# An interleaved second projection, per-token scales held in the constants' tile, and a head norm spread over the recurrence's tiles

## The reference, cut to what matters

```
h_lat = layernorm(x) * (1 + scale) + shift        # 512 tokens, x is the first block's RMS-normed output
h_ctx = the same for 256 context tokens           # computed earlier, loaded from memory
p = h @ w_in                                      # 5*512 columns get a 3x3 (or 3-tap) convolution,
                                                  # the rest: values mv, output gate mo, gates, low-rank lw, la, lg
out_m = sigmoid(mo) * headnorm(mLSTM(...))        # one mixer: chunkwise recurrence, both directions merged
out_r = (headnorm(rwkv7_scan(...)) + bonus) * g   # the other mixer: a second recurrence
x = layernorm(alpha * x + gate * ([out_m, out_r] @ w_out)) ...   # alpha = 2 ** 0.25
```

## Time and profile before

| | us |
|---|---|
| three runs, median (lowest to highest) | 3100.05 (3097.63 to 3113.56) |
| the profiled execution, its own time | 3105.09 |
| its span (first to last instruction) | 3102.8 |
| busy: PE / DVE / ACT / POOL | 2879.1 / 1863.6 / 1257.7 / 793.4 |
| second projection, first latent matmul to last copy's start | 1597.99 to 1850.70 |
| recurrence, first matmul to last sum | 2023.54 to 2369.89 |

### The profile page before, as it was taken

One profiled execution on the slowest core, in us unless ns is written; L12 is line 12 of the kernel. 1 busy time (PEld: TensorE's weight loads), 2 busy tenths in 40 slices (PEclk: granted clock), 3 DMA queues, 4 the chain that ended last, 5 costly groups with the idle time before them and its releaser, 6 DMA issues. The chain is left out here.

```text
span 3102.8 us, 55532 instructions
## 1 busy us (share of the span) xinstructions
PE 2879.1 (93%) x22953; PEld 2326.6 (75%) x22953; DVE 1863.6 (60%) x2647; ACT 1257.7 (41%) x1624; POOL 793.4 (26%) x461
## 2 busy tenths in 40 slices
PE   9889999999999989999989899768999799999994
PEld 7467888799777767888858677567886478888883
DVE  3766663210344445565257957785654789998997
ACT  3544322221333343332244312512222277777775
POOL 2013444344222203444400000010100125354431
PEclk9999999999999999999989899889999799999997
DMA  4633422332211112222222100321003379999996
GB/s 169 233 134 121 96 95 95 111 111 94 82 55 69 69 42 109 95 95 98 99 103 82 55 33 2 140 84 44 31 31 121 130 292 365 364 377 364 360 372 266
DMA packets 83397, 440.96 MB, mean 142 GB/s; under 512 B 19712, under 2 KB 22784, under 8 KB 34816
## 3 DMA queue, kind: packets, MB, share of 16 engines
q1 hardware_dynamic: 73920, 429.63, 38.2%
q0 software_dynamic: 9280, 8.43, 0.8%
HBM read 423.30 MB, written 37.77 MB: 149 GB/s over the span
## 5 line engine op out<-in xcount | busy, mean ns | idle before, releaser
L85 POOL TENSOR_TENSOR ring_lo<-ring,unit_hi 128x2048 fp32r<-128x2048 f32 x110 | 507.2, 4611 | 1047.5 <-ACT unit_hi L74 1047.5
L146 PE MATMUL wide<-h_hi,unit_hi 128*128 128x512 f32 x1296 | 516.7, 399 | 13.4 <-DVE h_lo L566 5.0
L148 PE MATMUL wide<-h_hi,ring_lo 128*128 128x512 f32 x1296 | 507.7, 392 | 0.0
L147 PE MATMUL wide<-h_lo,unit_hi 128*128 128x512 f32 x1296 | 507.0, 391 | 0.0
L3317 DVE TENSOR_TENSOR ex_w_lo<-ring,ex_w_hi 128x2048 fp32r<-128x2048 f32 x194 | 442.1, 2288 | 48.4 <-ACT ex_w_hi L3312 47.3
L3312 ACT CAST ex_w_hi<-ring 128x2048 fp32r<-128x2048 f32 x194 | 369.5, 1908 | 120.0 <-DMA ring<-in_weights 106.3
L74 ACT CAST unit_hi<-ring 128x2048 fp32r<-128x2048 f32 x114 | 217.6, 1909 | 389.6 <-PE wide L148 384.4
L146 PEld LDWEIGHTS wide<-h_hi,unit_hi 128*128 128x128 f32 x1296 | 245.0, 189 | 73.8 <-issue 15.2
L148 PEld LDWEIGHTS wide<-h_hi,ring_lo 128*128 128x128 f32 x1296 | 244.8, 189 | 52.5
L147 PEld LDWEIGHTS wide<-h_lo,unit_hi 128*128 128x128 f32 x1296 | 245.4, 189 | 49.1 <-issue 0.2
L391 DVE TENSOR_TENSOR ffn_hidden_lo<-ffn_whole,ffn_hidden_hi 128x512 f32 (+1 forms) x44 | 201.3, 4575 | 51.0 <-ACT ffn_hidden_hi L366 51.0
(11 more groups left out here) (560 smaller groups left out, 5770.5 us busy)
## 6 DMA issues: line engine op xcount, KB each, us to landing
ring<-in_weights SPq DMA_DIRECT2D x356, 1024.0 KB, 6.1
rw_F<-factors SPq DMA_DIRECT2D x8, 1024.0 KB, 6.0
factors<-rp_out SPq DMA_DIRECT2D x4, 1280.0 KB, 5.3
factors<-rp_out SPq DMA_DIRECT2D x4, 1024.0 KB, 5.1
ex_both<-pair_rows_out SPq DMA_DIRECT2D x4, 1024.0 KB, 7.8
x<-in_x SPq DMA_DIRECT2D x8, 256.0 KB, 7.0
x_kept<-x SPq DMA_DIRECT2D x1, 2048.0 KB, 12.2
x<-x_kept SPq DMA_DIRECT2D x1, 2048.0 KB
```

What stands on the lines that cost most here:

```text
L85: pool.tensor_tensor(self.lo[n % RING][:, :], self.ring[n % RING][:, :], self.hi[n % 2][:, :].bitcast(F32), ALU.subtract).then_inc(self.lo ...
L146: pe.matmul(dst, a[0], b[0], start=start, stop=False)
L147: pe.matmul(dst, a[0], b[1], start=False, stop=False)
L148: return pe.matmul(dst, a[1], b[0], start=False, stop=stop)
```

## The change

1. *Entry.* The four clearings go to POOL. The first low half of the weights is written before the variance. The variance's root comes first. The power of x is not inverted as a 128x512 tile: TensorE transposes it (four transposes in bank 7), ScalarE takes the root of four columns, one for each token tile, into `c.x_cols`, which lies in columns of the constants' tile that are not used any more, and VectorE inverts them and multiplies by alpha. x is scaled by the gain alone, by ScalarE, behind chunk `lw` (`gains`), and by the column much later in place of L3126's alpha.
2. *Projection.* The order of the chunks is `mixed`, `lw`, `conv` 0 and 1, then `mo` or `lg` and `conv` by turns, then `conv` 7 to 19 (`PROJECTED`); the weights are packed in that order. The context matmuls of chunks 0 and 1 come before the latent ones, and those are interleaved over k with h's low halves. Units are cast and their low halves written one item earlier. The gates' arithmetic starts at chunk 6. The values no longer wait for the copy of the last chunk and use banks 6, 7, 0 to 3; the gates' transposes use banks 4 and 5.
3. *Recurrence.* The head norm of the other mixer moves to tiles 1 to 4, one token tile in each: four parts behind slots 1 to 4, the root in slot 10, the scaling behind slot 11. The 16 transposes are in slot 14 and the mixes in slots 16 and 17 of tile 5. `starts` of tile 1 waits for masked pairs of tile 0 in place of the mixes; the last chain waits for the mixes. The squares use U[0] in place of base[0].

```diff
     def tensor(self, pe):          # Entry
+        pe.wait_ge(self.power_ready, 1)
+        for t in range(TT):
+            mm = pe.transpose(self.c.bank[7][:, t * P:(t + 1) * P], self.x_scale[:, t * P:(t + 1) * P], self.c.ident[:, :])
+        mm.then_inc(self.power_turned, 1)
     def scalar(self, act, between):
         between()
-        act.wait_ge(self.power_ready, 1)
-        act.activation(self.x_scale, self.x_scale, ACT.Sqrt).then_inc(self.power_root_ready, 1)
         act.wait_ge(self.var_ready, 1)
         act.activation(self.z_scale, self.z_scale, ACT.Sqrt).then_inc(self.var_root_ready, 1)
+        act.wait_ge(self.power_turned, 1)
+        act.activation(self.c.x_cols, self.c.bank[7][:, 0:T:P], ACT.Sqrt).then_inc(self.power_root_ready, 1)
+    def gains(self, act):
+        for k in range(DC):
+            act.activation(self.x[:, k, :], self.x[:, k, :], ACT.Copy, scale=self.gain(k)).then_inc(self.x_ready, 1)
...
-GATES_AT = 1
+GATES_AT = 6
+PROJECTED = [("mixed", 0), ("lw", 0), ("conv", 0), ("conv", 1)]
+for m, kind in enumerate(("mo", "mo", "mo", "mo", "lg")):
+    PROJECTED += [(kind, m % MC), ("conv", m + 2)]
+PROJECTED += [("conv", m) for m in range(7, CONV_CHUNKS)]
...
+            for n in range(2):                         # tensor: context first, then latent by k
+                for k in range(DC):
+                    block(n, unit, k, con(n), context)
+            for k in range(DC):
+                pe.wait_ge(entry.h_lo_ready, k + 1)
+                for n in range(2):
+                    mm = block(n, unit, k, lat(n), latent)
...
-                if n >= 2 and n % 2 == 0:              # scalar
-                    w.write_hi(act, 0, n // 2 + 1)
+                if n % 2 == 1:
+                    w.write_hi(act, 0, n // 2 + 2)
...
+                while following <= min((n + 1) // 2 + 1, U_IN_COLUMNS):      # vector
+                    w.write_lo(dve, 0, following)
+                    following += 1
...
-                        pe.wait_ge(mixed_ready, MC)    # rwkv, starts of tile 1
+                        pe.wait_ge(pair_masked[d], NH)
...
-                            elif at == 12:
+                            if p == TAT - 1 and at == 14:
                                 turn_hidden()
...
-                            if p == 0:
-                                if at in (2, 4, 6, 8):
-                                    center_hidden(at // 2 - 1)
...
+                            if 1 <= p <= TT:
+                                if 1 <= at <= 4:
+                                    center_hidden(p - 1, at - 1)
+                                elif at == 11:
+                                    scale_hidden(p - 1)
+                            if p == TAT - 1 and at in (16, 17):
+                                for m in range(2 * (at - 16), 2 * (at - 16) + 2):
+                                    mix_hidden(m)
...
-                    act.mul(normed[:, n // 2, n % 2 * T:(n % 2 + 1) * T], c.bank[5][:, :], ALPHA)
+                    act.activation(normed[:, n // 2, n % 2 * T:(n % 2 + 1) * T], c.bank[5][:, :], ACT.Copy, scale=c.x_cols[:, n // 2:n // 2 + 1])
```

More of the change, by code:

```diff
@@ L1313, in vector @@
         dve.wait_ge(self.power_root_ready, 1)
-        dve.reciprocal(self.x_scale, self.x_scale).then_inc(self.x_scale_ready, 1)
+        dve.reciprocal(self.c.x_cols, self.c.x_cols).then_inc(self.x_scale_ready, 1)
         dve.wait_ge(self.x_scale_ready, 1)
[L1316 to L1319, removed]
+        dve.tensor_scalar(self.c.x_cols, self.c.x_cols, ALPHA, None, ALU.mult).then_inc(self.x_scale_ready, 1)
 ORDER = ([0, 1, 2, 3, 4, 5], [1, 0, 5, 4, 3, 2])
@@ L1437, in tensor @@
             a, t = n // TAT, n % TAT
-            pe.matmul(c.bank[6 + n // 9][:, n % 9 * GR:(n % 9 + 1) * GR], self.g.rows[a][0:GR, t * P:(t + 1) * P],
+            pe.matmul(c.bank[4 + n // 9][:, n % 9 * GR:(n % 9 + 1) * GR], self.g.rows[a][0:GR, t * P:(t + 1) * P],
                       c.ident[0:GR, 0:GR], start=True, stop=True).then_inc(self.turned, 1)
 def project_in_stage(nc, c, w, h, u, pads, entry, gates, constants):
-    items = [("mixed", 0), ("lw", 0), ("lg", 0)] + [("mo", m) for m in range(MC)] + [("conv", m) for m in range(CONV_CHUNKS)]
-    CONV_FIRST = len(items) - CONV_CHUNKS
+    items = PROJECTED
+    VALUE_BANKS = [c.bank[n] for n in (6, 7, 0, 1, 2, 3)]
     chunk_done, copied, convolved, v_copied_act, v_copied_dve, silu_done, ones_written, constants_loaded, blank, *rest = c.semaphores(
@@ L1499, in _, with block @@
             entry.tensor(pe)
+            def block(n, unit, k, dst, toks):
+                b = (n % 2 * DC + k) * P
+                return product(pe, dst, [part[:, b:b + P] for part in unit], [part[k][:, toks] for part in h], k == 0, k == DC - 1)
+            latent, context = slice(CTX, TA), slice(0, CTX)
+            unit = w.parts(pe, 0, 0)
+            pe.wait_ge(entry.loaded, 16 * len(entry.loads))
+            for n in range(2):
[5 more added lines that the diff above has]
+                    mm = block(n, unit, k, lat(n), latent)
+                    if k == DC - 1:
+                        mm.then_inc(w.used if ends[n] else chunk_done, 1)
             for n, (kind, m) in enumerate(items):
+                if n < 2:
+                    continue
                 if n % 2 == 0:
                     unit = w.parts(pe, 0, n // 2)
+                if n == 3:
+                    pe.wait_ge(entry.power_root_ready, 1)
                 if n >= 4:
                     pe.wait_ge(copied, n - 3)
-                parts = [(lat(n), slice(CTX, TA))]
-                if kind in ("mixed", "lw") or kind == "conv" and not latent_only(m):
-                    parts.append((con(n), slice(0, CTX)))
+                parts = [(lat(n), latent)] + ([(con(n), context)] if kind == "conv" and not latent_only(m) else [])
                 for dst, toks in parts:
-                    if n == 0 and toks.start == 0:
-                        pe.wait_ge(entry.loaded, 16 * len(entry.loads))
                     for k in range(DC):
[L1513 to L1516, removed]
+                        mm = block(n, unit, k, dst, toks)
                 mm.then_inc(w.used if ends[n] else chunk_done, 1)
-            pe.wait_ge(copied, len(items))
+            pe.wait_ge(copied, len(items) - 1)
             for k in range(DC):
@@ L2505, in turn_hidden @@
                     pe.wait_ge(normed, TT)
+                    for d in both:
+                        pe.wait_ge(s_ready[d], TAT)
                     for m in range(MC):
@@ L3860, in second_block_units @@
         mixed[:, 32 * q:32 * q + NH] = gates[:, group * NH:(group + 1) * NH]
-    yield by_column_chunk(np.concatenate([mixed, lw_f, lw_b, lg, mo, w_in[:, :5 * DM], np.zeros((D, P), w_in.dtype)], 1))
+    chunks = {"mixed": mixed, "lw": np.concatenate([lw_f, lw_b], 1), "lg": lg, "mo": mo, "conv": w_in[:, :5 * DM]}
+    projected = [chunks[kind][:, m * P:(m + 1) * P] for kind, m in PROJECTED]
+    yield by_column_chunk(np.concatenate(projected + [np.zeros((D, P), w_in.dtype)], 1))
     yield by_row_chunk(mv)
```

122 lines of the change are left out of this document (62 added, 60 removed).

## The result

The changed kernel took 3078.1 us (median of 4 runs, 3075.4 to 3081.9) beside 3101.6 us for the kernel before on the same chip: a ratio of 0.9922 (95% interval 0.9896 to 0.9949), 23.5 us faster. A second set on another occasion gave 3073.2 us (6 runs) against 3103.6, ratio 0.9901 (0.9877 to 0.9924), 30.4 us faster. The forecast was 3068 with a range of 3057 to 3084.

What follows compares the result with a forecast made beforehand. TensorE, busy 93% of the span, was taken as the bound, so gains come from its waits and slow stretches. Projection 20.7 plus net recurrence 12.2 is 32.9 us off 3100.05: forecast 3068, range 3057 to 3084 for 8 in 10.

Steps and rivals of the forecast that it cites:

- Entry: Before the projection: weight half 0 and memsets leave the variance's way, and its root goes first; gain 0.5 us.
- rival C: Projection: the context part doesn't run early, held by transposes or loads, costing 5.7 us; 3074 us in all; chance 0.05.
- The queue walk: Projection, engine queues followed in program order: TensorE idles 15.3 us, the stage ends at 1830 against 1850.7, gain 20.7 us.
- the low clock after the 4.8 wait is eaten by the next one: Projection, behind unit 12's wait: slow matmuls there cost nothing extra; only 2.6 us charged behind the later 7.4 us wait.
- A delay at the gains passes 1:1 to the end: Projection: any delay at ScalarE's eight gains on x (4.8 us in all) lengthens the stage by as much.
- rival A: VectorE's queue eats more of the projection: walk off by 8 us, first pair 4 later; 3080 us; chance 0.18.
- Tile 0: Recurrence: 14 slots fall from 37.9 to 22.2 us without the norm, 2.5 of it allowed for low clock; gain 15.7.
- Tiles 1 to 4: Recurrence: the norm's parts fit VectorE's idle times and cost nothing; 16 us if all were exposed.
- rival B: The norm parts are exposed in the recurrence's tiles 1 to 4: 16 us dearer, 3084 us; chance 0.06.
- Tile 5: Recurrence: sixteen transposes take 2.0 us and the mixes lengthen their slots by 0.65 each; cost 3.5 us.
- rival D: Projection: TensorE's clock stays low, 0.20 us more per 512-column matmul; 3107 us with fifteen chunks; chance 0.04.
- faster by more: Whole kernel under 3084.5 us, beyond 0.5%: forecast, a larger-gain rival, nearly all of rival A, half of rival B; 0.89.

Runs made afterwards that it cites:

- the mean of six: Six profiles of kernels holding the changed recurrence: it takes 323.0 to 329.0 us, mean 325.6, against 335.3 and 335.4 with the old recurrence.
- the fill: Chunk 0's context part computed twice and tile 5's mixes one per step, against the kernel with norm centring also in tile 0: 3059.1 us, ratio 0.9856.
- the gates early: Changed kernel with the gates' VectorE arithmetic moved from behind conv 10 to 14 to behind conv 1 to 5: 3057.7 us, ratio 0.9862.
- The three small edits: Added in turn to the gates early: gains behind conv 0's copies (3059.9 us); norm centring in tile 0 (3057.4); repeated context matmuls with mixes spread out (3059.1).
- the burst: 1512 independent matmuls (64, 8, 256 columns) before the recurrence, added to the gates early with gains behind conv 0's copies; 8 and 64 columns: 29 ns per recorded matmul.
- steps of 1.60 us: Two useless VectorE products in each of tile 0's steps 1 to 12, added to the gates early with gains behind conv 0's copies: thirteen steps 21.9 us against 20.6.

## Why the prediction was right, point by point

It had the direction, the main mechanisms and the range right; the gain was put at 32.9 us and is 23.5 and 30.4 in two sets. Summed from stretches it is 0.4 + 17.7 - 0.7 (the same in both profiles of the changed kernel) + 9.8 (the mean of six) = 27.2. The 5.7 us that are missing from 32.9 are 2.5 in the projection, 2.4 in the recurrence, 0.7 between the two and 0.1 in the entry.

- **Entry**: 0.5 said, 0.4 measured. The context part ran in the wait for the low half, so rival C is out. The first pair of chunks was put at 1608.3, or 1605.7 with this execution's head start of 2.6 us, and ended at 1607.8 (its last matmul starts at 1607.37): the prediction named the low clock as the risk, at 3 to 4 us; it was 1.6, shown by the fill that removed it.
- **The queue walk**: every late unit was named in its place. Idle 15.3 said, 11.5 measured (unit 13 did not wait). The failed step is "the low clock after the 4.8 wait is eaten by the next one": it cost 2.3 us, and the one before the values 2.5. With 0.6 for the three modelled ends and the start behind unit 3, waits and clock together are 16.9, for 17.9 said. So the waits are not where the shortfall lies. It is the pair, 2.1 us late, and about 1.2 us that the walk's unit prices lack; the walk over the kernel before fell short by 3.7, and I did not take that off.
- **"A delay at the gains passes 1:1 to the end"**, under rival A: wrong, 2.2 of 4.9 us. In program order VectorE has 14 us of idle time behind it, and the walk did not list it. Listing it would also have shown that the gates belong there.
- **Tile 0**: 22.2 us for 14 steps, measured 22.8, but for another reason, so that its closeness is luck. The clock allowance of 2.5 was not needed: the granted clock is 1.00 in tile 0, against 0.78 from 2036.7 to 2076 before. In its place stand four stalls, 4.0 us by the excess of their steps. Three more, 2.9 us, fall in the tile's last six steps, where nothing was charged, so this profile gains 12.6 instead of 15.7 (13.9 on average).
- **Tiles 1 to 4**: "nothing" holds for the norm's parts, as the kernel without them shows. In tile 4 the steps 1.34, 2.96 and 2.85 became 1.46, 2.84 and 2.85: what sticks out of the first one is taken back in the second, as the prediction said. VectorE idles 12 to 17 us in the first 12 steps of each tile, so that sign of being wrong is not met, and rival B is out. The 3.1 us that these tiles seem to have lost lie within the scatter of equal code; 1.8 of them are TensorE's stalls, which the prediction did not know of.
- **Tile 5**: the transposes' step is 3.30 us, 1.96 over 1.34 (2.0 said), and the two steps with mixes 0.65 longer each, as said. Together 3.3; the nineteen steps grew by 2.55 only, since the kernel before has 0.6 more in one of them already. At the same granted clock tile 5 is 2.3 longer on average; over the six profiles it is 1.1, because the clock stands at 1.00 in two of them. That the recurrence as a whole comes near its forecast (9.8 = 13.9 - 3.1 - 1.1, rounded, for 12.2 = 15.7 - 0 - 3.5) is thus in part luck.
- **The clock (rival D)**: out in size. It is 0.89 from 1750 to 1780 and 0.83 from 1780 to 1800, else 1.00, and 0.98 over the whole 1620 to 1790, so the sign "below 0.9" is not met. The price of this rival was wrong: fifteen chunks of 24 matmuls at 0.20 more are 72 us, and so about 3140 and not 3107.
- **The total's base**: a median of three with 16 us between its extremes. Before's median was 3099.4 to 3103.6 in the later sets.
- **The chances**: the four terms named for "faster by more" add up to about 0.92, not 0.89.

The Trainium skill (ScalarE: Activation LUTs, "Table sets: the hidden batching unit") prices a table switch at about 2.7 us; the changed profile has 1.28 for each load again. The load ahead of the tanh starts 0.02 us behind the cast before it and the tanh 0.01 us behind the load, so nothing longer is hidden there:

```profile
1614.07 1.28 ACT L1593 ACT_TABLE_LOAD   x1
1615.36 0.60 ACT L1593 ACTIVATE lw<-wide 128x512 f32<-128x512 f32 x1
```

## What to carry to other kernels

List the idle times of the engine that is late, in program order, beside its full stretch: work that stands in the full stretch and whose inputs are ready at the idle one is worth more than its own length, here 14 us of work for 15.9, since each wait of TensorE also brings slow matmuls. With the gates early the kernel beats the changed one by 15.9 us in the trace, and by the totals too (ratio 0.9862 to before, against 0.9922 and 0.9901 in the two sets; with the second set the intervals just overlap). The three small edits on top of it (3057.4 to 3059.9) can't be told from it. And judge a part by a stretch inside one profile, repeated: the projection repeats to 0.07 us over three profiles, the totals scatter by 10. Before a difference of a few us in one stretch is given a cause, see how far equal code scatters there: tiles 1 to 4 scatter by 5.9.

## What the runs showed of the hardware

- In the recurrence's dependent small matmuls TensorE stood still 125 to 127 recorded matmuls behind the last such stall, or a multiple of that, for 0.2 to 1.9 us each in these two kernels, named "issue" in the profile: 6.2 us in tile 0 and 14.2 in tiles 1 to 4 of the changed kernel, 0.6 and 12.9 before. In the first 14 steps of tile 0 before, 2.7 us long on average, there was none; with steps of 1.60 us the stalls took less than with 1.34 (1.1 against 3.2 us over thirteen steps).
- The granted clock fell to 0.50 while the burst's 8-column matmuls ran without a pause (753 recorded in 40 us), and was back at 1.00 in the 256-column part. At full clock the recorded matmuls of 8 and of 64 columns both started 29 ns apart.
- A pause of 2.86 us was followed by eight matmuls at the lower clock, pauses of 4.53 and 6.14 us by 11 and 12; with the pause filled there were none.
